# Routed experts on one core: the gate half of the last three chunks of the first product is multiplied ahead of their up half

## The reference, cut to what matters

```python
def clamped_swiglu(hgu):
    gate, up = jnp.split(hgu, 2, axis=-1)
    gate = jnp.minimum(gate, SWIGLU_LIMIT)                  # 7.0
    up = jnp.clip(up, -SWIGLU_LIMIT, SWIGLU_LIMIT)
    return gate * jax.nn.sigmoid(SWIGLU_ALPHA * gate) * (up + 1)   # 1.702

def expert_block(args):
    xb, e = args
    return clamped_swiglu(xb @ w1[e] + b1[e]) @ w2[e] + b2[e]
```

## Time and profile before

| | |
|---|---|
| median of three runs | 2306.31 us |
| lowest, highest | 2303.6, 2308.85 us |
| profiled execution, span | 2306.2 us |
| mean granted clock of TensorE | 0.993 of full speed |
| TensorE busy (matmul) | 2209.2 us, 96% |
| VectorE busy | 1194.8 us, 52% |
| ScalarE busy | 650.0 us, 28% |
| first products (line 3060) | 2304 instructions, 514.1 us |
| second products (line 3108) | 1152 instructions, 255.4 us |
| loads of expert chunks | 384 of 1024 KB, median 16.1 us from issue to landing |

### The profile page before, as it was taken

How to read it: one execution, slowest core, us unless ns; L and a number is a source line. 1 busy time by engine, 2 the same in 40 slices (tenths; PEclk the granted TensorE clock), 3 DMA queues, 4 the chain that set the end, 5 groups by cost and what they waited for, 6 DMA issues and landing times. The chain is left out here.

```text
span 2306.2 us, 29645 instructions
## 1 busy us (share of the span) xinstructions
PE 2209.2 (96%) x10363; PEld 1188.4 (52%) x10364; DVE 1194.8 (52%) x2716; ACT 650.0 (28%) x1658; POOL 101.8 (4%) x234
## 2 busy tenths in 40 slices
PE   8999899999999999999999899999999999999997
PEld 3546685478744578777878633333333323333332
DVE  4989468453895563636745453334343333334334
ACT  3018442443221363336333321111111111111112
POOL 0001000000000051002001000000000000000000
PEclk9999999999999999999999999999999999999999
DMA  9670035301477103331241599989989998998998
GB/s 398 250 291 34 1 146 191 110 1 45 175 266 278 39 2 110 110 110 38 74 147 37 231 373 421 421 357 421 422 365 422 421 421 366 421 421 366 421 421 335
DMA packets 110280, 569.68 MB, mean 247 GB/s; under 512 B 11857, under 2 KB 13649, under 8 KB 51441
## 3 DMA queue, kind: packets, MB, share of 16 engines
q1 hardware_dynamic: 110192, 568.54, 61.6%
HBM read 567.46 MB, written 1.05 MB: 247 GB/s over the span
## 5 line engine op out<-in xcount | busy, mean ns | idle before, releaser
L3060 PE MATMUL PS<-BIG,PW 128*64 128x512 f32 x2304 | 514.1, 594 | 15.3 <-DMA BIG<-in_w 14.7
L3060 PEld LDWEIGHTS PS<-BIG,PW 128*64 128x64 f32 x2304 | 161.6, 137 | 353.6 <-issue 301.9
L3312 DVE TENSOR_SCALAR PW<-PS 128x512 f32<-128x512 f32 x36 | 24.9, 692 | 494.6 <-PE PS L3060 494.6
L3108 PE MATMUL PS<-BIG,PW 128*64 128x512 f32 x1152 | 255.4, 595 | 8.6 <-ACT PW L2923 8.6
L386 DVE SCALAR_TENSOR_TENSOR BIG<-BIG,COND_ROWS 128x1024 f32<-128x1024 f32 x128 | 153.4, 1221 | 24.9 <-DMA BIG<-in_w_ada_columns 24.6
L3108 PEld LDWEIGHTS PS<-BIG,PW 128*64 128x64 f32 x1152 | 79.2, 137 | 161.0 <-issue 142.7
L2900 ACT COPY BIG<-PS 128x512 f32<-128x512 f32 x37 | 21.7, 586 | 486.6 <-PE PS L3032 486.6
L1148 PE MATMUL PS<-HT,BIG 128*128 128x512 f32 (+1 forms) x448 | 152.0, 501 | 0.0
L1148 PEld LDWEIGHTS PS<-HT,BIG 128*128 128x128 f32 x448 | 85.1, 190 | 65.3 <-issue 60.3
L658 PE MATMUL PS<-HT,BIG 128*128 128x256 f32 x512 | 111.6, 379 | 1.4 <-PEq L863 1.4
L1553 PE MATMUL PS<-BIG,HT 128*128 128x512 f32 x256 | 110.0, 592 | 0.0
(11 more groups left out here) (547 smaller groups left out, 3171.6 us busy)
## 6 DMA issues: line engine op xcount, KB each, us to landing
BIG<-in_w SPq DMA_DIRECT2D x384, 1024.0 KB, 16.1
BIG<-in_l_w_ada_columns SPq DMA_DIRECT2D x40, 1024.0 KB, 7.2
BIG<-in_l_w_in SPq DMA_DIRECT2D x19, 2048.0 KB, 8.5
BIG<-in_w_ada_columns SPq DMA_DIRECT2D x24, 1024.0 KB, 7.1
BIG<-in_l_w_out SPq DMA_DIRECT2D x8, 2048.0 KB, 8.5
BIG<-in_w_in SPq DMA_DIRECT2D x7, 2048.0 KB, 8.1
BIG<-in_l_w_ada SPq DMA_DIRECT2D x4, 2048.0 KB, 17.9
BIG<-in_w_out SPq DMA_DIRECT2D x2, 2048.0 KB, 7.8
```

Of the source, the lines that this page charges most:

```text
L3060: ins = nc.tensor.matmul(PS[64 * g:64 * g + 64, 4 + half, :], xt[:, c % 4, c // 4, :], W[:, c, half * F + g * 512:half * F + g * 512 + 512 ...
L3108: ins = nc.tensor.matmul(PS[64 * g:64 * g + 64, 7, :], at_[:, k % 4, k // 4, :], W[:, 8 + k // 2, k % 2 * D + g * 512:k % 2 * D + g * 512 ...
```

## The change

Chunks 0 to 4 are as before. For chunks 5, 6 and 7 the kernel waits for each landing and multiplies only the gate half, then signals `gate_summed`, and then multiplies the up halves of 5, 6 and 7 with a `used` signal behind each. The functions `half_products` and `chunk_here` are only names for what stood in the loop. `beside` is called behind chunks 0 to 4 alone; no caller does anything behind a later one.

```diff
-                        for c in range(8):
+                        def half_products(c, half):
+                            for g in range(2):
+                                ins = nc.tensor.matmul(PS[64 * g:64 * g + 64, 4 + half, :], xt[:, c % 4, c // 4, :],
+                                                       W[:, c, half * F + g * 512:half * F + g * 512 + 512], start=False, stop=(c == 7),
+                                                       skip_group_check=True)
+                            return ins
+
+                        def chunk_here(c):
                             if piecewise:
                                 pe.wait_ge(loop["xt_copied"], c + 1)
                             pe.wait_ge(chunk_landed[c], load * 16 + 16)
-                            for half in range(2):
-                                for g in range(2):
-                                    ins = nc.tensor.matmul(PS[64 * g:64 * g + 64, 4 + half, :], xt[:, c % 4, c // 4, :],
-                                                           W[:, c, half * F + g * 512:half * F + g * 512 + 512], start=False, stop=(c == 7),
-                                                           skip_group_check=True)
-                                if c == 7 and half == 0:
-                                    ins.then_inc(loop["gate_summed"], 1)
-                            ins.then_inc(used, 1)
+
+                        for c in range(5):
+                            chunk_here(c)
+                            half_products(c, 0)
+                            half_products(c, 1).then_inc(used, 1)
                             if beside is not None:
                                 beside(c)
+                        for c in range(5, 8):
+                            chunk_here(c)
+                            ins = half_products(c, 0)
+                        ins.then_inc(loop["gate_summed"], 1)
+                        for c in range(5, 8):
+                            half_products(c, 1).then_inc(used, 1)
```

## The result

The changed kernel takes 2325.05 us (median of four runs, 2318.86 to 2330.32) against 2307.58 us before (four runs, 2303.6 to 2309.55): a ratio of 1.0079, 95% interval 1.0059 to 1.0099, so +17.5 us. The direction was as predicted, the size was not: 8.6 us were forecast, and the range ended at 2321. The profiled execution spans 2321.4 us, 15.2 us more than that of before.

The account below looks back on a forecast made before the run. The prediction took the experts' stage as a ring of transfers and TensorE, closed five times. Work behind the landings +8.6 us, gate signal, late release and clock 0 each: 2306.3 + 8.6 = 2314.9 us, range 2309 to 2321.

Parts of the forecast that it names:

- What bounds the kernel: Experts' stage: transfers and 14.5 us of TensorE alternate in a ring, closed five times by a landing of chunk 7.
- Step 2, the work behind the last landing: Five ring-closing blocks: four halves instead of one chunk left after chunk 7 lands, +1.72 us each, 8.6 us in all.
- Step 1, the earlier gate signal: Activation: gate clip can begin 1.72 us earlier, but the sigmoid is already hidden; taken as 0, at most 1.6 us gained.
- Step 3, the late release: After restarts: chunks 5 and 6 released 1.72 and 0.86 us later, covered by 2.5 us of queue; 0, at most 6.9.
- Step 4, the clock: TensorE's waits for chunks 5 to 7 in closing blocks: clock may fall, 1.7 us each; taken as 0, far end 8.5.
- rival A: Clock falls in the thin stretches of most closing blocks, three to five falls: 2320 to 2323 us; chance 0.12.
- B: After a restart, the later releases starve the transfer queue: up to 2321.8 us; chance 0.03.
- C: The later end of a closing block is hidden in the 14.5 us behind it: 2306.3 to 2308 us; chance 0.09.
- D: Sigmoid ends the activation in every block, so TensorE's 0.20 us ahead of the transposes goes: 2299 us; chance 0.04.

Follow-up runs that it names:

- e11: Kernel before, with the up columns of w1 not loaded for experts 1 to 31, so no wait for a transfer is left: 2283.70 us.
- e12: Changed kernel, with the up columns of w1 not loaded for experts 1 to 31: 2281.69 us.
- e9: Kernel before, with the gather moved behind chunk 7 and the sigmoid ahead of ScalarE's copy: ratio 1.0033 to before, +7.6 us.
- e2: Kernel before, order of products unchanged, chunk 5 signalled as used only together with chunk 6: ratio 1.0016 to before, +3.7 us.
- e14: Second profile of the kernel of e2 (order of before, chunk 5 released with chunk 6): ratio 1.0016 to before, +3.7 us.
- e6: Changed kernel, with the gather behind chunk 5's gate half instead of behind chunk 3: ratio 1.0069 to before, +15.9 us.
- e15: Second profile of the kernel of e6 (changed kernel, gather behind chunk 5's gate half): ratio 1.0069 to before, +15.9 us.
- e3: Changed kernel plus one unused filler product behind the gate halves of chunks 5 and 6, in every block but the first: ratio 1.0174 to before, +40 us.
- e4: Kernel before, with chunk 7 loaded by two transfers, gate columns first, each with its own wait: ratio 1.0004 to before, no change.

## Why the prediction was wrong, by its own steps

*What bounds the kernel*: right. Five closing landings, at the places named; each with sixteen matmuls behind it; no loss where no landing is waited for (e11, e12).

*Step 2, the work behind the last landing*: right in mechanism and size for four of the five places. 16.19 to 16.20 us for 14.48 is the +1.72 that was forecast, and e9 puts the same 1.72 there with other work and gets +7.6 us. At the first place little came: the stretch to the first restart varies by 1.7 us in the kernel before itself, and grew by 0.6 in the mean. There TensorE and the landing are nearly tied (two of the three profiles of before have no wait at chunk 7 there), so the term was worth 7.5 by the ledger, about 8.1 with the slow start of one profile of before taken out, and not 8.6.

*Step 1, the earlier gate signal*: right, 0.

*Step 3, the late release*: wrong. I took 0 because chunk 5 landed 8.0 us after its issue and the first chunk 5.5, and read the 2.5 us between as a queue that covers 1.72 us of delay. It does not: the transfers ran below their rate for some microseconds, chunk 5 landed up to 1.9 us later behind chunk 4 than it did before, and R-L grew by 2.8 us (2.9 and 4.2 in e2 and e14, which do nothing else). The failed reading is to take "in flight" for "at full rate". After the second restart of the changed kernel chunk 5's transfer was issued at about 1721.9 and chunk 4's landed at about 1725.0, so one was always in flight, and still the share of the engines sank to 0.75 from 1723.84 to 1725.84. How much is lost goes in part with how long chunk 4 was still under way when chunk 5 was issued. In the 28 restarts of changed, e2, e14, e6 and e15 it was 2.9 to 3.5 us in 13, and these lost 0.1 to 1.9 us, 1.2 in the mean; in the 15 with 3.6 to 4.5 us the loss was 0 to 1.0, 0.3 in the mean. What makes chunk 4 land sooner or later was not settled, nor why one transfer in flight does not hold 421 GB/s.

*Step 4, the clock*: wrong, and the larger miss. I saw two falls in the earlier trace rows, one of them with TensorE busy 54% of the time, priced a fall at 1.7 us, and still took 0 and gave rival A 0.12, because those were short matmuls. The price was right (1.3 to 1.7 us measured at each fall on the path); the count was 3, 3 and 2 in the three profiled executions, 4.0 us an execution in the mean. The argument from matmul length had no row behind it. The table above has what counts here: two thin stretches in a row gave 13 falls in 32 waiting blocks, one gave 1 in 32, none gave 0 in 67. e6 and e15 fill one of the two and keep the rest, and had 0 in 23. What decides between a fall and none in blocks of the same shape is open. "TensorE: Matmul & The Clock Gate", section "HAM oscillation — how this bites in real kernels", of the Trainium skill describes bursts between transfer waits that let the clock fall again and again; the trace agrees in that, with idle times of 1.22 and 1.40 us around a half of 0.86. The Trainium skill's own example has longer waits, some 3 to 5 us, and a fall at each of them; here they are shorter and it fell in 13 of 32 blocks. The prediction left the length of those waits out when it applied the rule to each closing block.

*The rivals*: A, the clock, took place in part and B, the release, too. I had priced them one by one, each as an alternative to the forecast, and so the range ended at 2321; together the terms reach 2306.3 + 7.5 + 4.0 + 2.8 = 2320.6, just inside the range. The measured 2325.05 lies 4.4 us above that. Of these 1.3 are the base, since the median of before moved from 2306.31 to 2307.58 us with its fourth run; the other 3.2 are the difference between the 14.3 us of the ledgers and the measured 17.5, inside the interval and with no cause shown. The prediction also took the profiled execution of before and the median run for the same time. A run's time is 1.8 us more than its span throughout the record, so that execution, with a span of 2306.2, took about 2308.0 us; the +8.6 does not hang on it. C and D did not happen.

## What to carry to other kernels

Work deferred past a wait is not free time used: if the wait is the one that the transfers set, everything deferred stands behind it, once per place where the bound changes hands, and the place can be found as a piece of the chain that starts at a landing. Before moving work out of a waiting stretch, ask what the engine's clock does while the stretch is thin, and what the buffers released later were about to feed; here these two cost as much again as the work itself (4.0 and 2.8 us for 6.9). And add up the side costs in the range: they come together, because they have one cause.

## What the runs showed of the hardware that was not expected

- A product on one group of 64 columns costs 0.86 us for 512 columns in two passes, and so does a pair on both groups (a half): in e3 each single product lengthened the block by 0.86. The two groups of a half run beside each other, and leaving one out saves nothing.
- With one 1 MB transfer per expert cut in two halves of 512 KB, the last landing of each ring came 0.4 to 0.7 us later than in the mean of before (e4, one profile; one and the same distance varies by up to 1.4 between the profiles of before).
- A transfer issued 3.1 us before the one ahead of it landed followed it by 4.4 us instead of 2.48 (second restart of the changed kernel).
- The clock fell in four or five of ten or eleven waiting blocks of the same shape in one execution, and in the next one in nearly but not exactly the same ones.
